# Sixteen attention steps in eighteen consecutive places, and some splits and waits in another order, in a three-block transformer kernel

## The reference

```python
u = h @ w_in
q, k, v, cb, cc, ch, g_conv, g_attn = jnp.split(u, splits, axis=-1)
y_conv = (cb * _causal_dwconv(cc * ch, conv_w)) @ w_conv_out        # 3 taps
for g, (window, dilation) in enumerate(DILATION_GROUPS):            # 3 groups of 8 heads
    o_g, lse_g = _dilated_window_attention(q[:, :, g], k[:, :, g], v[:, :, g], tab, window, dilation)
alpha = jax.nn.softmax(jnp.stack(lses, axis=0), axis=0)
o = jnp.sum(alpha[..., None] * jnp.stack(outs, axis=0), axis=0)
y_attn = o.reshape(B, S, ATTN_OUT).astype(h.dtype) @ w_attn_out
merged = jax.nn.sigmoid(g_conv) * y_conv + jax.nn.sigmoid(g_attn) * y_attn
return merged @ w_o
```

```python
xr = causal_conv(xr, conv_w[l], conv_b[l])
hr = rg_lru(xr, rg_a_w[l], rg_a_b[l], rg_x_w[l], rg_x_b[l], lru_lambda[l])
y_a = (hr * jax.nn.gelu(xg)) @ w_lru_out[l]
y_b = swa_sink_attention(q, k, v, attn_sinks[l], bias) @ w_attn_out[l]
g = jax.nn.sigmoid(u @ w_gate[l] + b_gate[l]).reshape(b, s, N_BRANCHES, d)
merged = g[:, :, 0] * y_a + g[:, :, 1] * y_b
```

## Time and profile before

| | |
|---|---|
| median of 3 runs | 2094.27 us (2092.14 to 2094.92) |
| profiled execution, its own time | 2095.6 us |
| its span, first to last instruction | 2093.5 us |
| mean granted clock of the matrix engine | 0.997 of full |
| busy: PE, PEld | 98%, 86% |
| busy: DVE, ACT, POOL | 68%, 49%, 2% |
| DMA traffic | 208 GB/s over the span |

### The profile page before, as it was taken

The page is one execution under the profiler, slowest core; times in us unless marked ns, Lnnn a source line. Parts: engine busy times, 40 slices in busy tenths (PEclk is TensorE's granted clock), DMA queues, the critical chain, the costliest instruction groups (busy, mean ns, idle before and its releaser), DMA issues.

```text
span 2093.5 us, 28979 instructions
## 1 busy us (share of the span) xinstructions
PE 2059.9 (98%) x11649; PEld 1790.4 (86%) x11649; DVE 1432.5 (68%) x1822; ACT 1028.6 (49%) x1279; POOL 36.3 (2%) x78
## 2 busy tenths in 40 slices
PE   7999999999999999999999999999999999999998
PEld 7788888999888888888899998888788799998887
DVE  5887788668777677767866786455654669656454
ACT  4443544444554363445444445444644668646443
POOL 0000000000000000000000000000000010000000
PEclk9999999999999999999999999999999999999999
DMA  9787698447678748868865496654755454456652
GB/s 316 258 283 251 193 290 253 128 139 253 230 256 267 245 168 277 264 202 260 287 183 145 143 300 192 203 188 141 234 188 183 135 160 137 161 183 210 192 190 80
DMA packets 355929, 438.04 MB, mean 209 GB/s; under 512 B 9571, under 2 KB 323371, under 8 KB 355796
## 3 DMA queue, kind: packets, MB, share of 16 engines
q1 hardware_dynamic: 350592, 420.51, 61.7%
q0 software_dynamic: 4160, 14.23, 3.1%
q10 hardware_dynamic: 1044, 1.46, 0.2%
HBM read 435.05 MB, written 1.11 MB: 208 GB/s over the span
## 4 chain that ended last, share of the span: by engine, by line
PE 88%; DVE 5%; ACT 4%; issue 1%; DMA 1%; DVEq 1%; SPq 0%; ACTq 0%
PE PC L1808 7%; PE PC L1810 7%; PE PC L1809 7%; PE PA L1808 6%; PE PA L1810 6%; PE PA L1809 6%; PE PB L1808 6%; PE PB L1810 6%; PE PB L1809 6%; PE PA L1801 4%; PE PA L1802 4%; PE PA L1803 4%; PE PC L1839 3%; PE PC L1976 2%; PE PC L1801 2%; PE PC L1803 2%
## 5 line engine op out<-in xcount | busy, mean ns | idle before, releaser
L1172 DVE TENSOR_TENSOR lo<-raw,hi 128x2048 fp32r<-128x2048 f32 x274 | 626.7, 2289 | 209.5 <-ACT hi L696 208.4
L696 ACT ACTIVATE hi<-raw 128x2048 fp32r<-128x2048 f32 x277 | 529.3, 1912 | 260.1 <-PE PC L1810 114.8
L1198 DVE SCALAR_TENSOR_TENSOR acc<-raw,cs,acc 128x256 f32<-128x256 f32 x448 | 217.2, 485 | 34.4 <-issue 0.9
L1808 PE MATMUL PA<-hi,nn 128*128 128x512 f32 (+1 forms) x528 | 210.3, 398 | 7.0 <-DVE nn L1274 5.9
L1801 PE MATMUL PA<-nn,hi 128*128 128x256 f32 x720 | 209.0, 290 | 0.4 <-ACT f L1089 0.4
L1810 PE MATMUL PA<-hi,nn 128*128 128x512 f32 (+1 forms) x528 | 206.0, 390 | 0.0
L1809 PE MATMUL PA<-lo,nn 128*128 128x512 f32 (+1 forms) x528 | 205.5, 389 | 0.0
L1802 PE MATMUL PA<-nn,lo 128*128 128x256 f32 x720 | 203.6, 283 | 0.0
L1803 PE MATMUL PA<-nn,hi 128*128 128x256 f32 x720 | 203.6, 283 | 0.0
L1808 PE MATMUL PB<-hi,nn 128*128 128x512 f32 x400 | 158.2, 395 | 0.5 <-DVE nn L1274 0.5
L1810 PE MATMUL PB<-hi,nn 128*128 128x512 f32 x400 | 156.6, 391 | 0.0
(11 more groups left out here) (317 smaller groups left out, 4088.8 us busy)
## 6 DMA issues: line engine op xcount, KB each, us to landing
raw<-in_w_in SPq DMA_DIRECT2D x90, 1024.0 KB, 5.4
raw<-in_ada_w SPq DMA_DIRECT2D x66, 1024.0 KB, 7.4
raw<-in_ffn_w_gate SPq DMA_DIRECT2D x88, 512.0 KB, 4.1
raw<-in_ffn_w_up SPq DMA_DIRECT2D x88, 512.0 KB, 5.2
raw<-in_ffn_w_down SPq DMA_DIRECT2D x44, 1024.0 KB, 5.2
raw<-in_ffn_w SPq DMA_DIRECT2D x88, 512.0 KB, 4.8
raw<-in_ffn_w SPq DMA_DIRECT2D x22, 1024.0 KB, 4.8
raw<-in_w_o SPq DMA_DIRECT2D x12, 1024.0 KB, 6.6
```

The costliest lines, as they stand in the source:

```text
L696: A(parts_of(n)[0], raw[:, n % 3, :], ACT.Copy).then_inc(hi_done, 1)
L1172: V.tensor_tensor(l, raw[:, n % 3, :], h.bitcast(F32), ALU.subtract).then_inc(lo_done, 1)
L1198: i = V.scalar_tensor_tensor(o, w[:, k, :], cs[:, k:k + 1], o, ALU.mult, ALU.add)
L1808: MM(o, xl, wh[:, c0:c0 + w], start=first, stop=False, skip_group_check=True)
```

## The change

Five things are moved; no work is added or taken away.

1. In block-1 mixers the sixteen steps run through: eighteen ticks (0 to 17) stand behind halves 3 to 20 (`TICK_AT1 = 3`), instead of four times six ticks behind halves 0 to 23. `chunk_T` of group o stands at half 9 + 4 o (`chunk_at`), the last of them at half 21; before, it stood at halves 6, 12 and 18 and in the tail.
2. In the same loop the splits keep their halves, but on ACT the copy of the second unit of a group and its split now come behind the tick of their half, and on DVE the split of a group's second unit stands behind the tick of half 6 j + 3.
3. In the block-2 mixer ACT's `split` comes before `gate2`, and in half 26 before `lru(3, 1)` as well. PE's `first_unit` waits for `sg_done` 18, the gate `gc` of half 26.
4. On DVE `lru(3, 3)` stands before `split(b+19)`.
5. In the change from stage 5 to 6, DVE's split stands before `final_norm(0)`.

```diff
--- before.py
+++ after.py
@@ -132,6 +132,14 @@
 def chunk_of(hu):
 
     return hu // 3 - 1 if hu % 3 == 2 and hu >= 5 else None
+
+
+TICK_AT1 = 3
+
+
+def chunk_at(hu):
+    c, r = divmod(hu - TICK_AT1 - 6, 4)
+    return c if r == 0 and 0 <= c < 4 else None
 
 
 def ada_no(p, u):
@@ -1015,28 +1023,27 @@
                         .then_inc(cH_done, 1)
 
                 def last_chunk():
-                    chunk_T(l * 4 + 3, 3, oH1)
                     conv_high(3)
 
-                for j in range(4):
-                    c = b + 18 + 3 * j
-                    if j:
-                        chunk_T(l * 4 + j - 1, j - 1, oH1)
-                    tick(1, st0, 4 * j, 0)
-                    tick(1, st0, 4 * j, 1)
-                    if j:
-                        conv_high(j - 1)
-                    after(c)
-                    A(f1[:, :], prod[0], ACT.Copy).then_inc(cv_act, 1)
-                    split(c + 3)
-                    tick(1, st0, 4 * j, 2)
-                    after(c + 1)
-                    A(f2[:, :], prod[1], ACT.Copy).then_inc(cv_act, 1)
-                    split(c + 4)
-                    tick(1, st0, 4 * j, 3)
-                    tick(1, st0, 4 * j, 4)
-                    after(c + 2)
-                    split(c + 5)
+                for hu in range(24):
+                    j, r = divmod(hu, 6)
+                    c, o = b + 18 + hu // 2, chunk_at(hu)
+                    if o is not None:
+                        chunk_T(l * 4 + o, o, oH1)
+                    if TICK_AT1 <= hu < TICK_AT1 + STEPS + 2:
+                        tick(1, st0, 0, hu - TICK_AT1, STEPS)
+                    if r == 1:
+                        if j:
+                            conv_high(j - 1)
+                        after(c)
+                        A(f1[:, :], prod[0], ACT.Copy).then_inc(cv_act, 1)
+                    elif r == 3:
+                        after(c)
+                        A(f2[:, :], prod[1], ACT.Copy).then_inc(cv_act, 1)
+                    elif r == 5:
+                        after(c)
+                    if r % 2:
+                        split(c + 3)
 
                 gates = {0: f1, 1: f2, 2: f1, 3: f2}
                 tail(s, TAIL_AT1, TAIL1, BANK1, lambda kind, j: gates[j] if kind == "ga" else f3, None,
@@ -1137,7 +1144,7 @@
                     recurrent_gates(j)
                 if i == 3 and 1 <= j < 4:
                     lru(j - 1, 2)
-                if i == 0 and j >= 1:
+                if i == 0 and 1 <= j < 4:
                     lru(j - 1, 1)
                 if i == 4 and 0 <= j < 4:
                     lru(j, 0)
@@ -1145,9 +1152,11 @@
                     after(b + 3 + u)
                     if SPREAD[u] == "q":
                         queries(u // 3 + 1, prod[(u + 1) % 2])
-                    elif SPREAD[u] in ("ga", "gc"):
+                    split(b + 6 + u)
+                    if i == 0 and j == 4:
+                        lru(j - 1, 1)
+                    if SPREAD[u] in ("ga", "gc"):
                         gate2(f1 if SPREAD[u] == "ga" else f2, SPREAD[u], 0, prod[1])
-                    split(b + 6 + u)
                 if i == 1 and j == 4:
                     lru(j - 1, 2)
 
@@ -1337,8 +1346,8 @@
                 elif s == 5:
                     add_gated(s, 0)
                     midway()
+                    split(BASE[s + 1])
                     final_norm(0)
-                    split(BASE[s + 1])
                     lows(Aq, 0, (0,))
                     add_gated(s, 1, (0,))
                     lows(Aq, 0, (1,))
@@ -1619,32 +1628,31 @@
                                     ALU.subtract)
 
                 def last_chunk():
-                    chunk_T(l * 4 + 3, 3, oH1, oL1)
                     conv(3, (0, 1, 2))
                     conv_low(3)
 
-                for j in range(4):
-                    c = b + 18 + 3 * j
-                    if j:
-                        chunk_T(l * 4 + j - 1, j - 1, oH1, oL1)
-                    tick(1, st0, 4 * j, 0, l * 4)
-                    if j:
+                for hu in range(24):
+                    j, r = divmod(hu, 6)
+                    c, o = b + 18 + hu // 2, chunk_at(hu)
+                    if o is not None:
+                        chunk_T(l * 4 + o, o, oH1, oL1)
+                    if TICK_AT1 <= hu < TICK_AT1 + STEPS + 2:
+                        tick(1, st0, 0, hu - TICK_AT1, l * 4, STEPS)
+                    if r == 0 and j:
                         conv(j - 1, (0, 1))
-                    tick(1, st0, 4 * j, 1, l * 4)
-                    if j:
+                    elif r == 1 and j:
                         conv(j - 1, (2,))
                         conv_low(j - 1)
-                    tick(1, st0, 4 * j, 2, l * 4)
-                    split(c + 3)
-                    tick(1, st0, 4 * j, 3, l * 4)
-                    split(c + 4)
-                    tick(1, st0, 4 * j, 4, l * 4)
-                    after(c + 2)
-                    dve.wait_ge(cv_act, (l * 4 + j + 1) * 2)
-                    V.tensor_tensor(cpad[:, :, 4:], prod[2].rearrange("p (c t) -> p c t", c=2),
-                                    f2[:, :].rearrange("p (c t) -> p c t", c=2), ALU.mult)
-                    tick(1, st0, 4 * j, 5, l * 4)
-                    split(c + 5)
+                    elif r == 2:
+                        split(c + 2)
+                    elif r == 3:
+                        split(c + 3)
+                    elif r == 5:
+                        after(c)
+                        dve.wait_ge(cv_act, (l * 4 + j + 1) * 2)
+                        V.tensor_tensor(cpad[:, :, 4:], prod[2].rearrange("p (c t) -> p c t", c=2),
+                                        f2[:, :].rearrange("p (c t) -> p c t", c=2), ALU.mult)
+                        split(c + 3)
 
                 gates = {0: f1, 1: f2, 2: f1, 3: f2}
                 tail(s, TAIL_AT1, TAIL1, BANK1, lambda kind, j: gates[j] if kind == "ga" else f3,
@@ -1778,8 +1786,8 @@
                     chunk_T(8 + c, c, oH2, oL2)
 
             def last_chunks():
+                lru(3, 3)
                 split(b + 19)
-                lru(3, 3)
 
             tail(7, TAIL_AT2 + 3, TAIL2[3:], BANK2[3:], gate_home2, mH2, mL2, m322, ya2, False, 8, 19, last_chunks,
                  None)
@@ -2131,22 +2139,24 @@
                         gate_sums(s)
                 st0 = l * STEPS
                 pe.wait_ge(gate_rdy, s + 1)
-                for j in range(4):
-                    c = b + 18 + 3 * j
-                    for u in range(3):
-                        arrive(c + u)
-                        half(c + u, prod[u], 0, nh, nl)
-                        if u == 0 and j:
-                            chunk_T(l * 4 + j - 1 if j > 1 else None, (j - 1) % 2, st0 + 4 * j)
-                        if j == 0 and u == 0:
-                            pe.wait_ge(qk_done, 12 * (l + 1))
-                        tick(1, st0, 4 * j, 2 * u, v1, l * 4 + j if j else None)
-                        half(c + u, prod[u], 1, nh, nl).then_inc(unit_done, 1)
-                        tick(1, st0, 4 * j, 2 * u + 1, v1)
+                for hu in range(24):
+                    u, m = divmod(hu, 2)
+                    c, o, k = b + 18 + u, chunk_at(hu), hu - TICK_AT1
+                    if m == 0:
+                        arrive(c)
+                    i = half(c, prod[u % 3], m, nh, nl)
+                    if m:
+                        i.then_inc(unit_done, 1)
+                    if o is not None:
+                        chunk_T(l * 4 + o if o else None, o % 2, st0 + 4 * o + 4)
+                    if k == 0:
+                        pe.wait_ge(qk_done, 12 * (l + 1))
+                    if 0 <= k < STEPS + 2:
+                        tick(1, st0, 0, k, v1, l * 4 + o + 1 if o is not None else None, STEPS)
 
                 def first_unit(k, o):
+                    pe.wait_ge(cv_act, l * 8 + 8)
                     unit(k, o, nh, nl)
-                    chunk_T(l * 4 + 3, 1, st0 + 16)
 
                 tail(s, TAIL_AT1, TAIL1, BANK1, oH1, oL1, True, first_unit, 4, l * 4 + 4)
                 out_proj(s, mH1, mL1, l * 4)
@@ -2222,6 +2232,7 @@
 
             def first_unit(k, o):
                 pe.wait_ge(ol_done, 16)
+                pe.wait_ge(sg_done, 18)
                 unit(k, o, oH2, oL2)
 
             def first_recurrent(k, o):
```

## The result

| | before | after |
|---|---|---|
| median of 7 runs each, us | 2093.28 (2092.14 to 2094.92) | 2101.09 (2098.95 to 2101.96) |
| profiled execution, own time, us | 2095.6 | 2101.1 |
| its span, us | 2093.5 | 2099.3 |

The change makes the kernel slower by 0.34%: the ratio is 1.0034, with a 95% interval of 1.0025 to 1.0043. That is 7.8 us between the medians; the ratio is one of the means of the seven runs, and by it the difference is 7.1 us.

A forecast was written before the change was run, and what follows sets the result against it. PE, busy 98% of the span, was taken as the bound. +1.6 us for both block-1 mixers, +3.0 for stage 7 and +2.5 for the clock made +7.1, a predicted median of 2101.3 us, range 2094 to 2106.

The forecast's parts named there:

- The start: First steps of each block-1 mixer: wait for `k` goes, -1.15 us; scores of step 2 come 0.7 late, +0.9 in all.
- The steady steps: Packed steps of the block-1 mixers: no new waits, taken as 0; fewer interruptions of PE, -0.1 us per mixer.
- Rival B: Packed steps overload DVE and late splits recur at every group: adds 4 us to the sum, 2105.3; chance 0.12.
- The tail: End of each block-1 mixer: PE waits 2.0 us before units 33 and 34 instead of 0.9, +1.1 us.
- Stage 7: Block-2 mixer: PE waits for gates, net +0.8 at half 24, +5.2 before the first tail unit, -3.0 behind: +3.0 us.
- Rival C: Faster: waits aimed at go, none replaces them, gate `gc` done by 1801.4; -4.7 us, 2089.6; chance 0.13.
- The clock: Behind PE's 5.2 us wait in stage 7 the granted clock falls for 3.4 to 6.8 us of dense work: +2.5 us.
- rival A: No fall of the clock in stage 7: +4.6 us in all, 2098.9; chance 0.2.
- Parts 4 and 6: The block-2 mixer's waits in stage 7, +3.0 us, and the clock's fall there, +2.5 us.
- The split ahead of `final_norm(0)`: Change from stage 5 to 6: DVE is idle on both sides, 0 us, bounds -0.2 to +0.5.

The follow-up runs named there:

- Run 6: run 1 with ACT's copy and split of a group's second unit put back ahead of the tick: 2094.87 us, ratio 0.9997 to the kernel before.
- run 1: The kernel before with only the block-1 mixers changed, stage 7 and the change from stage 5 to 6 left alone: 2095.45 us, ratio 1.0008.
- Run 3: The changed kernel with PE's wait for the gate `gc` moved from tail unit 17 to unit 18: 2097.59 us, ratio 1.0017 to the kernel before.
- run 2: The kernel before with only stage 7 changed (splits before gates, PE's wait for `gc`, `lru(3, 3)` before the split): 2099.0 us, ratio 1.0025.
- run 5: The kernel before with only DVE's split put ahead of `final_norm(0)`: 2093.58 us, ratio 0.9997.
- run 7: run 1 with DVE's tail reordered (last group's convolution before the first `ada`, second `ada` behind unit 34's split): 2095.47 us, ratio 0.9999 to the kernel before.
- run 8: The kernel before with the same new order of DVE's tail as run 7 and nothing else: 2101.84 us, ratio 1.0030.
- run 4: The kernel before with only `lru(3, 3)` put ahead of the split of unit 19 on DVE: 2092.14 us, ratio 0.9993.
- run 10: run 8 with SP's modulation loads of the tail each one weight load later: 2096.49 us, ratio 1.0013 to the kernel before.

## Why the prediction was right

The mechanism was right at each place. The terms of the waits were off by little; the clock's term came near by two errors that cancel.

- **The start.** The wait for `k` went, and the scores of step 2 wait in its place: 0.70 late for 0.7, and 0.20 at the transposes, 0.90 for 0.9 predicted. Run 6 shows that ACT's order makes it.
- **The steady steps.** No wait in any group, as taken. Rival B falls: packed steps don't overload DVE.
- **The tail.** 1.56 and 0.53, for "1.5 and 0.5"; the chain from unit 29 took 25.12 us for 25.1, since it lost `oL` alone, and PE came early. A mixer costs 0.86, for 0.8, and run 1 puts both at 1.7 for 1.6.
- **Stage 7.** Before half 24, 2.42 for "over 2"; before the first tail unit 5.05 for 5.2; none at step 14's product or at unit 18. The waits together add 2.8, for 3.0. Unit 17 could start at 1802.77 and the gate was done at 1807.72, where the prediction had 1801.4 and 1806.45. Both are 1.3 later, behind the unforeseen fall of the clock, so the wait between them came out right. Run 3 shows that most of the 5.05 comes from the place of the wait; 2.2 us of it come back at unit 18. Rival C falls: `gc` ended at 1807.72, not by 1801.4.
- **The clock.** It fell, so rival A falls, and for 6.8 us. Its term was 2.5, and the clock cost 3.0, but not as summed. A fall of 3.4 us that was not in the sum came behind the 2.4 us wait, in one of three profiles with that wait, and cost 1.5 (run 2 against the whole change). The fall that was in the sum cost the other 1.5 and not 2.5, since 2.8 of its 6.8 us passed while PE was still waiting. That the total is near is luck. The fall of the earlier trace rows, which I took for fixed, differs from run to run. Parts 4 and 6 together said +5.5 for stage 7, and the trace says +5.8.
- **The split ahead of `final_norm(0)`** is worth nothing that shows (run 5, and the same two waits in both traces).

The sum was +7.1; the medians say +7.8, the ratio +7.1, with an interval of 5.2 to 9.0. The time of 2101.3 against 2101.09 measured is nearer than the sum deserves: before's median over the seven runs was 2093.28, 1.0 lower than that of the first three, and this took back the 0.7 that the sum lacked against the medians.

What I had not seen, and what only the experiments taught, is how much the waits of the tail are worth if they are moved well: my own repairs of it (runs 7 and 8) were costed by DVE's chain alone. The step in them that failed is that the next splits would be ready: I had not followed SP's queue past the moved `ada`, nor, in run 8, the wait of 3.41 us for `oL` ahead of it.

## What to carry to other kernels

Moving work away from a place leaves every chain that was anchored there uncovered: follow, on each engine, what now runs there without company, and the loads that wait for a buffer it frees. A wait belongs right before the first instruction that needs it: one matrix unit too early cost some 3.5 us here. Judge a repair together with the order it is for, since the same tail gained 4.4 us on one order and lost 2.7 on the other.

## What the runs showed of the hardware

- **The clock's falls come and go between executions of the same stretch.** At the change to stage 7 four of the fourteen profiles had no fall (those of runs 4, 5, 8 and 10), seven had 3.4 us in one piece or the first of two, and three had 6.8. The wait of 2.4 us in stage 7 (2.3 in its bracket) had a fall behind it in one profile and none in two (runs 2 and 3). A fall of 3.4 us is worth up to 1.7, so single profiles must not be subtracted without a look at it. How much of the spread of 2 to 3 us between runs comes from this is not shown: of the 31 runs of before that go with runs 1 to 4, the seven with a mean granted clock of 0.998 took 2094.0 on average, and the 23 with 0.999 and 1.000 took 2093.7.
- **A fall doesn't need a long wait.** In run 3 it came behind a wait of 2.0 us, in run 8 behind waits of 2.4 and 2.2, and in the profile after behind one of 2.3, in otherwise dense work. The Trainium skill, "TensorE: Matmul & The Clock Gate", section "Why this matters for your kernels", advises against idle gaps between bursts of matmuls; the falls at the waits of 2.0 to 5.05 us agree with it. The waits of up to 1.6 us in the block-1 mixers had none.
- **A table load costs 1.28 us and no more here.** The gate starts 1.29 us after its load does (1785.44 and 1786.73), and the load 0.02 us after the split ends.
- **SP's queue holds up other engines.** A load that waits for its buffer keeps back the loads behind it that wait for nothing: 6.03 us of idle time on ACT in run 7.
